# A decoder network on one NeuronCore: in the last attention layer, the next scores are issued ahead of the product of weights and values, in 11 of 16 steps

## The chip, the cores and the metric

The kernel runs on one core of one Trainium2 chip. The metric is the time of one execution on the device in microseconds, the median of several runs. The weights are loaded from HBM within the time.

## The reference, cut to what matters

The network has 256 tokens of 1024 channels and four mixers: a layer of two windowed attentions, one of forgetting attention, both with MLPs, an mLSTM, and last a sparse attention (NSA) with 16 heads of 64 in 4 groups. The change lies in the last one. With 256 tokens its selected and its windowed branch see all earlier keys, so each is causal attention with its own keys and values; the third branch attends to 15 compressed blocks. Their outputs are weighted by gates, added, multiplied by silu(z) and put through `w_out`:

```python
p_cmp = masked_softmax(jnp.einsum('bsghd,bcgd->bghsc', q, k_cmp) * scale, cmp_mask)
...
    p = masked_softmax(jnp.einsum('bqghd,bkgd->bghqk', qb, kb) * scale, mask)
    return jnp.einsum('bghqk,bkgd->bqghd', p.astype(vb.dtype), vb)
...
o = gate[..., 0:1] * heads(o_cmp) + gate[..., 1:2] * heads(o_sel) + gate[..., 2:3] * heads(o_win)
return (o.reshape(B, S, NSA_INNER) * jax.nn.silu(z)) @ w_out
```

All is float32. The kernel takes large products as three in rounded halves (high by high, high by low, low by high), and the attention's small products in float32.

## The kernel before, in words

The engines run programs of their own and meet at semaphores. Nothing reorders them: the order of the work is the order in which `pe`, `act`, `dve` and `pool` of the class `Nsa` are written.

The attention is cut into N = 16 steps. Step i holds the pair of heads j = i // 2 and the branch b = i % 2, with keys in two tiles of 128. One step passes through these stations:

- S, `score` (L2319, matmuls at L2328) on TensorE: the products of queries and keys, 4 instructions. Each contracts over 64 channels, so it takes half of the array's rows, and the two heads take one half each. The result goes to two PSUM banks, `SETS[i % 2]`, out of which the turned weights of step i - 2 must have been copied.
- `mask` (L2785, L2792) on VectorE: scale, causal mask and row maximum. It waits for the scores and keeps the masked scores in `nsa_sc`.
- `exp` (L2581, L2587) on ScalarE, with the row sum.
- `scale` (L2796, L2800 and L2806) on VectorE: by the sum's reciprocal and the gate.
- T, `turn` (L2333, L2337) on TensorE: six 128 x 128 transposes by a product with the identity, into the same banks.
- `keep` (L2590, L2595) on ScalarE: the copy of the turned weights into `nsa_pt`.
- V, `values` (L2341, L2352) on TensorE: weights times values, 4 instructions on all 128 rows and 64 columns each. In an odd step one more product follows, C (L2356): the compressed branch of the same heads, from `nsa_pc` and `nsa_vcmp`, over 64 rows. It closes the sum of the pair, and signals `summed`.
- `full` (L2825, L2830) on VectorE: the pair's y times silu(z), then `high` (L2601) on ScalarE and `low` (L2832, L2834) on VectorE, which split it for the output product.

In iteration k of the loop TensorE issues T(k), small products of the compressed branch where k % 4 is 3 or 1, half a chunk of projections or of the output product (`slot_half`, L2359, the matmuls of L189 to L191), V(k), and S(k + 2). V(k) and S(k + 2) both need `keep` of step k. S of steps 4, 8 and 12 also needs the turned queries of its group (`q_ready`): q is copied out behind slots 1, 5 and 9 (L2562), a DMA exchanges its halves (`nsa_qtwo`), VectorE multiplies and adds (L2731, L2738), and GpSimd multiplies the other part (L2513).

Beside this, ScalarE rounds the raw weight chunks to their high half (L155) and VectorE subtracts to get the low half (L159, L183); of four chunks GpSimd does the first half (L2505). In iteration k ScalarE does `exp(k + 1)` and then `keep(k)`, except in steps 6 and 10, where `keep` goes first. VectorE begins iteration k with `mask(k + 1)`; at even k from 2 on the gate product `full(k // 2 - 1)` follows, but `full(6)` stands at the end of iteration 13, and `low` behind it, ahead of `mask(15)`. After the loop TensorE finishes the output product, whose first matmul (L189) needs `low(6)`. In iteration 14 the output product waits for `full(6)` too.

Of the kernel before, what the change touches and what calls it, by code (L numbers as in the profile page):

```python
# [85 lines left out]
def build(nc, x, chunks, small_in, const_in, even_in, ml_in, nsa_in, fnorm_in, out):  # L86
# [100 lines left out]
    def product(pe, dst, a_hi, a_lo, b_hi, b_lo, start, stop):  # L187

        pe.matmul(dst, a_hi, b_hi, start=start, stop=False)  # L189
        pe.matmul(dst, a_hi, b_lo, start=False, stop=False)  # L190
        return pe.matmul(dst, a_lo, b_hi, start=False, stop=stop)  # L191

    def channel_tile(pe, slot, half, dst, h_hi, h_lo, ready=None):

        for k in range(KT):
            if ready is not None:
                pe.wait_ge(ready, k + 1)
            cols = slice(k * CW + half * P, k * CW + half * P + P)
            last = product(pe, dst, w_hi[slot][:, cols], w_lo[slot][:, cols],
                           h_hi[:, k, :], h_lo[:, k, :], k == 0, k == KT - 1)  # L200
        return last
# [26 lines left out]
    class Norm:  # L228
# [37 lines left out]
        def pe(self, pe):  # L266
            pe.wait_ge(self.diag_ready, TT)
            for k in range(KT):
                for t in range(TT):
                    at = (k % 2) * S + t * P  # L270
                    last = pe.matmul(bank[4 + k // 2][:, at:at + P], xres[:, t, k * P:(k + 1) * P],
                                     self.diag[:, t, :], start=True, stop=True)
                if k % 2 == 1:
                    last.then_inc(self.turned, 1)
# [1800 lines left out]
    class Nsa:  # L2075
# [354 lines left out]
        def pe(self, pe):  # L2430
            c0, inp = self.c0, self.inp
            first, rest = range(0, WIDE_KT), range(WIDE_KT, KT)
            pe.wait_ge(lo_ready, c0 + 1)
            pe.wait_ge(inp.lo_done.sem, inp.lo_done.at(WIDE_KT))
            for half in range(2):
                self.in_tile(pe, self.KC, half, bank[half][:, 0:S], first)
            inp.pe(pe, 1, self.before.added)
            pe.wait_ge(lo_ready, c0 + 2)
            for half in range(2):
                self.in_tile(pe, self.VC, half, bank[2 + half][:, 0:S], first)  # L2440
            pe.wait_ge(inp.lo_done.sem, inp.lo_done.at(KT))
            for half in range(2):
                last = self.in_tile(pe, self.KC, half, bank[half][:, 0:S], rest)
            last.then_inc(chunk_used, 1)
            pe.wait_ge(self.diag_ready.sem, self.diag_ready.at(TT))
            for t in range(TT):
                last = pe.matmul(bank[4][:, t * P:(t + 1) * P], ones, self.diag[:, t, :], start=True, stop=True)
            last.then_inc(self.rows_done.sem, 1)
            for half in range(2):
                last = self.in_tile(pe, self.VC, half, bank[2 + half][:, 0:S], rest)  # L2450
            last.then_inc(chunk_used, 1)
            pe.wait_ge(self.c_kept.sem, self.c_kept.at(1))
            self.in_whole(pe, self.KS, 0)
            pe.wait_ge(self.const_loaded.sem, self.const_loaded.at(16))
            self.gates(pe)
            self.in_whole(pe, self.KW, 1)
            pe.wait_ge(self.rows_kept.sem, self.rows_kept.at(1))
            pe.wait_ge(self.raw_kept.sem, self.raw_kept.at(1))
            self.in_whole(pe, self.Q[0], 0)
            pe.wait_ge(self.raw_kept.sem, self.raw_kept.at(2))  # L2460
            self.in_whole(pe, self.Z[0], 1)
            self.compress(pe, 0)
            self.compress(pe, 1)
            self.turn_gates(pe)
            self.values_half(pe, 0, 0)
            self.turn_hidden(pe, 0)
            self.values_half(pe, 0, 1)
            self.turn_hidden(pe, 1)
            pe.wait_ge(self.k_ready.sem, self.k_ready.at(2))
            pe.wait_ge(self.k_swapped.sem, self.k_swapped.at(4))  # L2470
            self.score(pe, 0)
            self.values_half(pe, 1, 0)
            self.compressed_keys(pe)
            self.compressed_values(pe)
            self.values_half(pe, 1, 1)
            pe.wait_ge(self.z_kept.sem, self.z_kept.at(1))
            self.score_compressed(pe, 0, 1)
            pe.wait_ge(self.cmp_kept.sem, self.cmp_kept.at(2))
            self.score(pe, 1)
            for k in range(self.N):  # L2480
                self.turn(pe, k)
                if k % 4 == 3 and k < 12:
                    self.score_compressed(pe, k // 4 + 1, 0)
                if k % 4 == 1:
                    self.turn_compressed(pe, k // 4)
                self.slot_half(pe, k)
                self.values(pe, k)
                if k + 2 < self.N:
                    self.score(pe, k + 2)
            for t in range(TT):  # L2490
                self.out_half(pe, 2, t).then_inc(self.t_done.sem, 1)
                if t == 1:
                    pe.wait_ge(lo_ready, self.o0 + 4)
                if t == 0:
                    self.out_half(pe, 3, t).then_inc(self.t_done.sem, 1)
            for i in range(2):
                self.out_quarter(pe, 3, i).then_inc(self.t_done.sem, 1)
# [1141 lines left out]
```

## Time and profile before

| | us |
|---|---|
| median of 3 runs | 932.59 |
| lowest and highest | 932.19, 932.75 |
| the profiled execution's own time | 932.07 |
| its span, first to last instruction | 930.2 |
| PE busy | 918.2 (99%) |
| DVE, ACT, POOL busy | 605.9, 561.9, 100.6 |
| first and last score matmul of this layer (L2328) | 810.3, 903.1 |
| PE's share of the chain that ended last | 89% |

PE is TensorE's matmuls, PEld its weight loads, DVE VectorE, ACT ScalarE, POOL GpSimd, SP the queue that issues most DMAs. The granted clock is 0.999 of full speed over the span. In a timeline a row gives the start, the time from the first start to the last recorded end, the engine, line, operation, tiles and shapes, how many instructions are merged, and in brackets how long the engine sat idle before and what it waited for. A float32 matmul stands as two records, one for each pass. "64*128" is an array use of 64 rows and 128 columns. The recorded ends of matmuls overlap the next starts, so distances are read from start to start.

### The profile page before, as it was taken

The numbers are of one execution on the slowest core, as the hardware profiler recorded it, in microseconds if no ns is written. First come the engines' busy times: TensorE is split into PE (matmuls) and PEld (weight loads), VectorE is DVE, ScalarE is ACT, GpSimd is POOL, SyncE is SP. The second block draws the span as 40 slices with busy tenths as digits, with TensorE's granted clock in tenths as the row PEclk, the third lists the DMA queues.
The fourth block names the chain that finished last, engine by engine and source line by source line (L and its number), as shares of the span: only waits on it lengthen the run. The fifth ranks groups of instructions, "written<-read, shape, count | busy, mean of one in ns | idle before, by whom it ended". The sixth has DMA issues, their size and how long they took to land.

```text
span 930.2 us, 15087 instructions
## 1 busy us (share of the span) xinstructions
PE 918.2 (99%) x6098; PEld 802.4 (86%) x6098; DVE 605.9 (65%) x1073; ACT 561.9 (60%) x927; POOL 100.6 (11%) x145
## 2 busy tenths in 40 slices
PE   9999999999999999999999999999999999999997
PEld 7876899998888877799998888999988889988876
DVE  6767676654456666666665454677479757777885
ACT  6687565553435787755555343656487547868873
POOL 0210000000000000000000016245003101311101
PEclk9999999999999999999999999999999999999999
DMA  9833565565554435236555565234333542731201
GB/s 362 322 139 125 181 213 194 182 213 194 181 184 173 149 128 181 69 142 228 197 182 212 195 221 184 95 130 140 138 139 106 227 172 99 266 118 53 99 24 46
DMA packets 23020, 153.57 MB, mean 165 GB/s; under 512 B 2632, under 2 KB 2888, under 8 KB 5544
## 3 DMA queue, kind: packets, MB, share of 16 engines
q1 hardware_dynamic: 22024, 149.17, 44.7%
q0 software_dynamic: 640, 3.15, 1.0%
q8 instruction: 48, 0.79, 0.3%
q10 hardware_dynamic: 288, 0.30, 0.1%
q14 instruction: 20, 0.16, 0.1%
HBM read 150.57 MB, written 1.05 MB: 163 GB/s over the span
## 4 chain that ended last, share of the span: by engine, by line
PE 89%; ACT 4%; DVE 4%; issue 1%; DMA 1%; SPq 0%; ACTq 0%; DVEq 0%
PE bank L189 26%; PE bank L191 25%; PE bank L190 25%; PE bank L931 1%; PE bank L2337 1%; PE bank L955 1%; PE bank L944 1%; PE bank L1610 1%; PE bank L2328 1%; PE bank L2352 1%; DVE w_hi_lo L159 1%; PE bank L761 1%; PE bank L1595 1%; ACT w_hi_lo L155 1%; DMA raw<-in_chunks 1%
## 5 line engine op out<-in xcount | busy, mean ns | idle before, releaser
L159 DVE TENSOR_TENSOR w_hi_lo<-raw,w_hi_lo 128x2048 fp32r<-128x2048 f32 x121 | 277.4, 2296 | 151.2 <-ACT w_hi_lo L155 151.1
L155 ACT ACTIVATE w_hi_lo<-raw 128x2048 fp32r<-128x2048 f32 x135 | 257.8, 1913 | 108.8 <-PE bank L191 107.4
L189 PE MATMUL bank<-h,w_hi_lo 128*128 128x256 f32 x960 | 270.0, 281 | 0.2 <-DVE ml_x L1872 0.2
L190 PE MATMUL bank<-h,w_hi_lo 128*128 128x256 f32 x960 | 266.2, 277 | 0.0
L191 PE MATMUL bank<-h,w_hi_lo 128*128 128x256 f32 x960 | 266.1, 277 | 0.0
L190 PEld LDWEIGHTS bank<-h,w_hi_lo 128*128 128x128 f32 x960 | 181.0, 188 | 0.4 <-issue 0.2
L189 PEld LDWEIGHTS bank<-h,w_hi_lo 128*128 128x128 f32 x960 | 180.4, 188 | 1.1 <-issue 0.7
L191 PEld LDWEIGHTS bank<-h,w_hi_lo 128*128 128x128 f32 x960 | 180.4, 188 | 0.0
L189 PE MATMUL bank<-w_hi_lo,mlp_u_hi 128*128 128x512 f32 x256 | 99.8, 390 | 0.0
L190 PE MATMUL bank<-w_hi_lo,mlp_u_hi 128*128 128x512 f32 x256 | 99.6, 389 | 0.0
L191 PE MATMUL bank<-w_hi_lo,mlp_u_lo 128*128 128x512 f32 x256 | 99.6, 389 | 0.0
L189 PE MATMUL bank<-w_hi_lo,h 128*128 128x512 f32 (+1 forms) x184 | 72.7, 395 | 0.3 <-DVE w_hi_lo L3354 0.3
L190 PE MATMUL bank<-w_hi_lo,h 128*128 128x512 f32 (+1 forms) x184 | 70.2, 381 | 0.0
L191 PE MATMUL bank<-w_hi_lo,h 128*128 128x512 f32 (+1 forms) x184 | 70.2, 381 | 0.0
L1214 ACT ACTIVATE mlp_work<-bank 128x256 f32<-128x256 f32 x64 | 21.1, 382 | 71.6 <-PE bank L191 71.6
L191 PEld LDWEIGHTS bank<-w_hi_lo,mlp_u_lo 128*128 128x128 f32 x256 | 48.1, 188 | 9.9
L189 PEld LDWEIGHTS bank<-w_hi_lo,mlp_u_hi 128*128 128x128 f32 x256 | 48.1, 188 | 9.9
L190 PEld LDWEIGHTS bank<-w_hi_lo,mlp_u_hi 128*128 128x128 f32 x256 | 48.1, 188 | 9.8
L769 ACT ACTIVATE h<-bank,small 128x256 fp32r<-128x256 f32 x48 | 18.8, 476 | 43.9 <-PE bank L761 43.9
L189 PEld LDWEIGHTS bank<-w_hi_lo,h 128*128 128x128 f32 x184 | 34.6, 188 | 10.5 <-issue 3.9
L191 PEld LDWEIGHTS bank<-w_hi_lo,h 128*128 128x128 f32 x184 | 34.6, 188 | 6.9
L190 PEld LDWEIGHTS bank<-w_hi_lo,h 128*128 128x128 f32 x184 | 34.7, 188 | 5.7
(397 smaller groups left out, 1434.2 us busy)
## 6 DMA issues: line engine op xcount, KB each, us to landing
raw<-in_chunks SPq DMA_DIRECT2D x136, 1024.0 KB, 4.9
even_bias<-in_even POOLq DMA_DIRECT2D x8, 384.0 KB, 3.4
xres<-in_x SPq DMA_DIRECT2D x2, 512.0 KB, 5.3
raw<-in_chunks SPq DMA_DIRECT2D x2, 512.0 KB, 6.4
ml_z<-in_ml SPq DMA_DIRECT2D x1, 896.0 KB, 5.8
nsa_qtwo<-nsa_qraw SPq DMA_DIRECT2D x8, 80.0 KB
small<-in_small SPq DMA_DIRECT2D x1, 559.5 KB, 11.9
final_gain<-in_fnorm SPq DMA_DIRECT2D x1, 512.0 KB, 3.6
```

Of the source, the lines that this page charges most:

```text
L155: act.activation(w_hi[slot][:, :], raw[slot][:, :], ACT.Copy).then_inc(hi_ready, 1)
L159: dve.tensor_tensor(w_lo[slot][:, :], raw[slot][:, :], w_hi[slot][:, :].bitcast(F32), ALU.subtract).then_inc(lo_ready, 1)
L189: pe.matmul(dst, a_hi, b_hi, start=start, stop=False)
L190: pe.matmul(dst, a_hi, b_lo, start=False, stop=False)
L191: return pe.matmul(dst, a_lo, b_hi, start=False, stop=stop)
L761: last = pe.transpose(self.spot(k)[:, t * P:(t + 1) * P], xres[:, t, k * P:(k + 1) * P], ident)
L769: act.activation(self.h[:, k, 0, :], self.spot(k), ACT.Copy, scale=self.gain[:, k:k + 1])\
L931: last = pe.matmul(bank[at_bank[e]][:, self.PS[t]:self.PS[t] + self.KEYS[t]], b["q"][half, t * P:(t + 1) * P], b["k"][half, 0:self.KEYS[t] ...
L944: last = pe.transpose(bank[self.banks_of[i % 2][e]][:, m * P:(m + 1) * P], self.sc[i % 2][:, e, at:at + P], ident)
L955: last = pe.matmul(dst[HALVES[e], kt * P:S], b["v"][e][kt], pt[:, e, kt * S:kt * S + S - kt * P], start=(kt == 0), stop=(kt == 1))
L1214: act.activation(self.z[n % 2][:, half * S:(half + 1) * S], self.up_bank(n, half)[:, 0:S], ACT.Copy).then_inc(self.z_ready.sem, 1)
L1595: last = pe.matmul(bank[5 + e][:, t * VW:(t + 1) * VW], self.X[:, j, t * P:(t + 1) * P], bdv[e][:, :], start=True, stop=True)
```

## The change

In iterations with k % 4 other than 2 and k + 2 < 16, S(k + 2) is issued ahead of V(k), behind a wait for the copy of step k. In iterations 2, 6 and 10, and in 14 and 15, the order stays. The other engines' programs are the same.

```diff
@@ -2484,9 +2484,14 @@
                 if k % 4 == 1:
                     self.turn_compressed(pe, k // 4)
                 self.slot_half(pe, k)
-                self.values(pe, k)
-                if k + 2 < self.N:
+                if k % 4 != 2 and k + 2 < self.N:
+                    pe.wait_ge(self.pt_ready.sem, self.pt_ready.at(k + 1))
                     self.score(pe, k + 2)
+                    self.values(pe, k)
+                else:
+                    self.values(pe, k)
+                    if k + 2 < self.N:
+                        self.score(pe, k + 2)
             for t in range(TT):
                 self.out_half(pe, 2, t).then_inc(self.t_done.sem, 1)
                 if t == 1:
```

TensorE at the end of iteration 1, from the end of slot 1 to the turn of step 2, before (each row an instruction, with the semaphores it waits for; `at_pt` is the copied weights, `ns_pc` the copied compressed weights, `at_scaled` the scaled ones):

```order
L191 MATMUL bank<-h,w_hi_lo 128x256
L2352 MATMUL bank<-nsa_pt,nsa_v 64x256 [waits at_pt]
L2352 MATMUL bank<-nsa_pt,nsa_v 64x256
L2352 MATMUL bank<-nsa_pt,nsa_v 64x128 x2
L2356 MATMUL bank<-nsa_pc,nsa_vcmp 128x256 [waits ns_pc]
L2328 MATMUL bank<-nsa_kd,nsa_qr 128x128 [waits at_pt]
L2328 MATMUL bank<-nsa_kd,nsa_qr 128x128
L2328 MATMUL bank<-nsa_kd,nsa_qr 128x256 x2
L2337 MATMUL bank<-small,nsa_sc 128x128 [waits at_scaled]
L2337 MATMUL bank<-small,nsa_sc 128x128 x5
```

The same place on TensorE now:

```order
L191 MATMUL bank<-h,w_hi_lo 128x256
L2328 MATMUL bank<-nsa_kd,nsa_qr 128x128 [waits at_pt]
L2328 MATMUL bank<-nsa_kd,nsa_qr 128x128
L2328 MATMUL bank<-nsa_kd,nsa_qr 128x256 x2
L2352 MATMUL bank<-nsa_pt,nsa_v 64x256 [waits at_pt]
L2352 MATMUL bank<-nsa_pt,nsa_v 64x256
L2352 MATMUL bank<-nsa_pt,nsa_v 64x128 x2
L2356 MATMUL bank<-nsa_pc,nsa_vcmp 128x256 [waits ns_pc]
L2337 MATMUL bank<-small,nsa_sc 128x128 [waits at_scaled]
L2337 MATMUL bank<-small,nsa_sc 128x128 x5
```

The scores moved past the values and past the compressed product, which now stands between the values and the turn; both still wait for the same copy, and the added wait gives no instruction of its own.

The second place is VectorE's program at the end of iteration 13 and the start of 14, which the change leaves as it is: the last scaling of step 14, half a chunk, the gate product `full(6)`, `low(5)`, and the mask of step 15 (`at_summed` is what V and C signal, `at_scores` what S signals):

```order
L2806 TENSOR_SCALAR nsa_sc<-nsa_sc,nsa_st,nsa_gate 128x256 x2
L183 TENSOR_TENSOR w_hi_lo<-raw,w_hi_lo 128x1024 [waits hi_ready]
L2830 TENSOR_TENSOR nsa_yf<-bank,nsa_sz 128x256 [waits at_ylo,ns_zready,at_summed]
L2834 TENSOR_TENSOR nsa_y_lo<-nsa_yf,nsa_y_hi 128x256 [waits at_yhi]
L2792 ISA nsa_sc,nsa_st<-bank,const 128x128 [waits at_turned,at_scores]
```

Nothing moved here, but on TensorE what `at_scores` stands for comes earlier and what `at_summed` stands for comes later.

## Rows read from the trace of the kernel before

**Rows 1.** The page, busy time, share of the span and instructions of TensorE

```profile
PE 918.2 (99%) x6098; PEld 802.4 (86%) x6098; DVE 605.9 (65%) x1073; ACT 561.9 (60%) x927; POOL 100.6 (11%) x145
```

**Rows 2.** Waits, 808 to 918 us: who waited for whom, us, times, longest

```profile
DVE nsa_sc L2792 <- PE bank L2328: 11.2, 11, 3.6
...
PE bank L2337 <- DVE nsa_sc L2806: 3.0, 3, 1.2
```

**Rows 3.** Timeline of TensorE, step 0: start us, us, engine line op

```profile
822.78 0.28 PE L190 MATMUL bank<-h,w_hi_lo 128*128 128x256 f32 x1
822.89 0.28 PE L191 MATMUL bank<-h,w_hi_lo 128*128 128x256 f32 x1
823.10 0.87 PE L2352 MATMUL bank<-nsa_pt,nsa_v 128*64 128x256 f32 x8
823.90 0.93 PE L2328 MATMUL bank<-nsa_kd,nsa_qr 64*128 64x128 f32 x8
824.76 0.87 PE L2337 MATMUL bank<-small,nsa_sc 128*128 128x128 f32 x6
```

**Rows 4.** Timeline of TensorE, steps 13 and 14

```profile
901.33 0.87 PE L2352 MATMUL bank<-nsa_pt,nsa_v 128*64 128x256 f32 x8
...
902.45 0.38 PE L2356 MATMUL bank<-nsa_pc,nsa_vcmp 64*128 64x256 f32 x1
...
906.96 0.87 PE L2352 MATMUL bank<-nsa_pt,nsa_v 128*64 128x256 f32 x8
907.76 0.88 PE L2337 MATMUL bank<-small,nsa_sc 128*128 128x128 f32 x6
```

**Rows 5.** Timeline of TensorE, step 1

```profile
829.63 0.48 PE L2356 MATMUL bank<-nsa_pc,nsa_vcmp 64*128 64x256 f32 x1
829.64 0.48 PE L2328 MATMUL bank<-nsa_kd,nsa_qr 64*128 64x128 f32 x2
...
830.91 0.87 PE L2337 MATMUL bank<-small,nsa_sc 128*128 128x128 f32 x6
```

**Rows 6.** Timeline of TensorE, step 15 and the output product behind it

```profile
912.24 0.70 PE L2356 MATMUL bank<-nsa_pc,nsa_vcmp 64*128 64x256 f32 x2
912.99 0.47 PE L189 MATMUL bank<-w_hi_lo,nsa_y_hi 128*128 128x512 f32 x1
```

**Rows 7.** Timelines of ScalarE, VectorE and TensorE ahead of steps 7 and 3

```profile
855.70 0.81 ACT L2595 ACTIVATE nsa_pt<-bank 128x768 f32<-128x768 f32 x1 [0.34 <-PE bank L2337]
856.53 1.28 ACT L2587 ACT_TABLE_LOAD   x1
...
861.24 0.87 PE L2337 MATMUL bank<-small,nsa_sc 128*128 128x128 f32 x6 [1.17 <-DVE nsa_sc L2806]
...
832.71 1.65 DVE L2731 TENSOR_TENSOR nsa_qtwo<-nsa_qtwo,nsa_csr 128x512 f32<-128x512 f32 x1 [0.48 <-DMA nsa_qtwo<-nsa_qraw]
...
836.91 0.88 PE L2337 MATMUL bank<-small,nsa_sc 128*128 128x128 f32 x6 [0.69 <-DVE nsa_sc L2806]
```

**Rows 8.** Timeline of VectorE, steps 13 to 15

```profile
903.10 0.42 DVE L2830 TENSOR_TENSOR nsa_yf<-bank,nsa_sz 128x256 f32<-128x256 f32 x1
...
903.76 0.29 DVE L2792 CUSTOM_DVE_ANT_0 nsa_sc<-bank,const 128x128 f32<-128x128 f32 x1
...
911.28 1.23 DVE L183 TENSOR_TENSOR w_hi_lo<-raw,w_hi_lo 128x1024 fp32r<-128x1024 f32 x1 [2.69 <-POOL w_hi_lo L2505]
912.42 0.42 DVE L2834 TENSOR_TENSOR nsa_y_lo<-nsa_yf,nsa_y_hi 128x256 fp32r<-128x256 f32 x1
```

**Rows 9.** Timelines of ScalarE and GpSimd, steps 14 and 15

```profile
905.87 0.79 ACT L2595 ACTIVATE nsa_pt<-bank 128x768 f32<-128x768 f32 x1
...
906.87 1.90 ACT L155 ACTIVATE w_hi_lo<-raw 128x2048 fp32r<-128x2048 f32 x1
...
908.84 2.40 POOL L2505 TENSOR_TENSOR w_hi_lo<-raw,w_hi_lo 128x1024 fp32r<-128x1024 f32 x1 [26.95 <-ACT w_hi_lo L155]
```

**Rows 10.** Timeline of TensorE's weight loads, the load of T in step 1

```profile
824.75 0.64 PEld L2337 LDWEIGHTS bank<-small,nsa_sc 128*128 128x128 f32 x6 [0.33 <-issue]
```

## The prediction

> **What bounds the kernel.** I read the page first: TensorE has a matmul in flight for 99% of the span [rows 1], and where it is busy throughout, only two things can change the time: the time of its own instructions, and the places where it waits. So the second view is the list of waits over the last stage. The change hopes for the first of its two rows: VectorE waited 11.2 us, in 11 places, for scores (L2328). But the row below it is the one that counts: TensorE itself waited for scaled weights (L2806) only 3 times, 3.0 us in all [rows 2]. VectorE's other waits are idle time of an engine with room to spare. The third view is TensorE's timeline at the block borders, because the edit alters only the order of three blocks: S (scores, L2328), V (weights times values, L2352, and in odd steps one product more, L2356, which I call C) and T (turning the next step's weights, L2337).
>
> **Even steps.** In step 0, V starts at 823.10, S at 823.90, T at 824.76 [rows 3]: from V's start to what follows it 0.80, from S's start to what follows it 0.86. These pitches include the change of block. If they belong to the block that goes before, as the same 0.80 from V straight to T in step 14 says (906.96 to 907.76, [rows 4]), S, V, T takes 0.86 + 0.80, what V, S, T took. Four of the 11 swapped steps are even (0, 4, 8, 12): price 0. If the pitch depended on the pair, the bounds would be the differences between these rows, 0.06 either way per step.
>
> **Odd steps.** Here C stood between V and S, and the records interleave: C starts at 829.63, S at 829.64, and T at 830.91 [rows 5]. C and S together take 1.28, S alone 0.86, so C costs 0.42 beside S. In the new order C stands between V and T. T uses all 128 rows of the array, C and each score 64. What C costs alone is seen in step 15, where nothing of S is left: it starts at 912.24 and the record of its two passes ends at 912.94 [rows 6]. T starts 0.07 before the recorded end of the 64-row block ahead of it (823.90 + 0.93 = 824.83 against 824.76, [rows 3]), so C alone takes 0.63: 0.21 more than beside S. The upper bound is the start of the next matmul, 912.99, hence 0.75 and 0.33 more, though that one also waits for VectorE (below). The lower bound is 0.42, no loss. I take 0.205, as the next matmul's own start is disturbed and the pass pair's end is not. The waits do not add to it: S now waits for the copied weights first (ScalarE, L2595) and V, which waited for the same copy, comes behind. A doubled wait on one semaphore is one wait, and no engine gets an instruction more.
>
> The Trainium skill, TensorEngine Tiling (Array Packing), section Key Properties, says that changing the tiling mode drains TensorE, and that different tiles may run in parallel. By it the odd steps have four mode changes between slot and T where they had three; at a price like the pitch from V to S less a normal one this would be about 0.1 per step, and the sum would be 0.5 us lower; that is an estimate. The trace says more than a drain: C alone against C beside S is 0.21 [rows 5, 6].
>
> **What the earlier scores buy.** S starts 0.80 sooner in even steps and 1.2 sooner in odd ones. This pays only where a T waits, in steps 3, 7 and 11. Take T(7): TensorE waited 1.17 for it and began at 861.24. Back from there: scaling, on the exponentials of step 7, behind a table load (856.53), behind ScalarE's copy of step 6's turned weights, from 855.70, which itself waited 0.34 for T(6) [rows 7]. The scores of step 7 are in none of these links. T(6) stands behind S and V in either order, so T(7) moves with T(6). T(11) repeats this. T(3), at 836.91, hangs on VectorE's product of 832.71 (L2731), which waited for the DMA that turns q [rows 7], and q is copied out behind slot 1, ahead of S and V. Gain: 0 in all three. It is also why the loss of step 1 costs nothing: T(3) starts at its time whatever happens in TensorE within its slack of 0.7. Should every score's lead reach T, the gain is bounded by 3.0 [rows 2].
>
> Steps 3, 5, 7, 9 and 11 keep their loss, as the waits behind them hang on T(6) and T(10), which are late too: 5 x 0.205 = 1.03 us.
>
> **The tail.** Here V's lateness meets an engine without slack. In step 13 VectorE multiplies y by the gate (L2830) at 903.10, just after the last product C of step 13 (V starts at 901.33; C's second pass ends at 902.45 + 0.38 = 902.83), and only behind it masks step 15's scores at 903.76 [rows 4, 8]. In the new order V starts at 901.33 + 0.86 = 902.19, C at 902.99, its second pass 0.32 later (912.94 - 0.38 - 912.24), at 903.31, with its end at 903.69. The gate product begins at about 903.73, 0.63 later, with the earlier scores of step 15 waiting behind it. All that follows is a chain: mask, exponentials, the copy of step 14 (905.87), rounding of the last weights (906.87), GpSimd's half of them (908.84 for 2.40), VectorE's other half (911.28), the low part of y (912.42), and TensorE's L189 at 912.99 [rows 6, 8, 9]. The output product of step 14 waits for the gate product too, and should just get it in time. On VectorE and GpSimd these stand back to back, so L189 moves from 912.99 to about 913.60, by 0.61. TensorE on its own would be later by 0.205 from step 13 and 0.2 from waiting for the copy of step 14 (906.96 + 0.205 against 907.36): 0.41 on 912.87, thus not the later of the two. From 912.99 on TensorE works through to the last blocks. Bounds: 0.2 (only C's loss) and 0.85 (the whole lead of S, 0.86).
>
> **Sum.** 1.03 + 0.61 = 1.64 us. On the profiled execution's 932.07 that is 933.7; its time is 0.52 below the median of 932.59, and on the median it is 934.2. A difference of 0.2% (1.87 us) is about what a measurement of this kernel tells from none; the forecast lies just inside, at 0.18%.
>
> **Rivals.** *C is dearer (0.12).* If C alone costs 0.75, each of the five steps loses 0.33 and the sum is 5 x 0.33 + 0.61 = 2.2 us: 934.8, slower by 0.24%. For it speaks the gap to 912.99, against it that VectorE's last row ends at 912.84, which leaves only its signal before 912.99. It decides from a price of 0.252 per step on: 5 x 0.252 + 0.61 = 1.87.
>
> *The tail is hidden (0.14).* ScalarE's chain before step 13 starts up to 0.8 earlier, and if some of that reached the mask of step 15, only 0.2 of the tail is left: 933.8; with no loss for C it is 932.8. Against it is the order of VectorE's rows: the mask stands behind the product that needs V.
>
> *The scores do pay (0.06).* If the waits of steps 3, 7 and 11 all vanish, -3.0 + 1.64 gives 931.2; without a loss for C, 930.2. Against it are the links of [rows 7].
>
> *Changes of block are free (0.04).* If TensorE loaded the next block's weights beside the running one, C alone would take two passes at the 0.11 pitch of the slot's matmuls of 256 columns (822.78 to 822.89, [rows 3]), 0.2 less than beside S, and every odd step would win 0.2: -1.0 + 0.4, 932.0. In the trace the weight load of T stands idle for 0.33 us before it starts behind S [rows 10]. The Trainium skill, TensorE: Matmul & The Clock Gate, section Step-by-step: what each phase is for, says that weight loads are pulled ahead of running matmuls when they go to the background buffer; that idle row says that here they are not.
>
> **How the numbers follow.** The forecast has 0.64, with a spread of its own of 933.7 to 934.7: a quarter of that, 0.17, is past 934.46 and counts as slower; with the first rival 0.29. Faster by over 0.2% (below 930.7) is only the last part of the third rival: 0.03. The rest, 0.68, is within 0.2%. The range reaches down to the second rival's end, 932.8, with 0.2 for the measurement, and up to the upper price with a longer tail, 5 x 0.33 + 0.85 = 2.5, 935.1.
>
> **What would show it.** Right: from slot to T about 2.5 us in odd steps (V, C and S took 2.08) with C alone between V and T, even steps unchanged at 1.66 to 1.67; waits before T(3) shorter by 0.2, before T(7) and T(11) as before; VectorE idle before L2830 in step 13, and about 0.6 us idle on TensorE or its weight load around steps 14, 15 and the L189 behind them; VectorE's waits for scores fewer. Wrong: T(7) or T(11) without a wait, C at 0.42 in its new place, or the mask of step 15 at its old distance from T(14).

## The result: 0.16% slower, and the profile after

| | before | after |
|---|---|---|
| median, us (22 runs each, same chip) | 932.45 | 933.90 |
| lowest and highest | 931.73, 932.90 | 933.45, 934.53 |
| ratio of the times, with its 95% interval | | 1.0016 [1.0010, 1.0022] |
| the profiled execution's own time | 932.07 | 933.72 |
| its span | 930.2 | 931.9 |

The difference of the medians is 1.45 us, that of the profiled executions 1.65; the forecast was 1.64, within 0.2%.

The page of the kernel after, busy time by engine [rows 1]; the granted clock is 0.998 over the span:

```profile
PE 919.8 (99%) x6098; PEld 801.9 (86%) x6098; DVE 605.9 (65%) x1073; ACT 561.6 (60%) x927; POOL 99.3 (11%) x145
```

The same instructions on every engine; TensorE's busy time is 1.6 longer, and the others' is the same within 1.3. Behind the edit all line numbers are 5 higher (VectorE's mask is L2797, its scaling L2811, the gate product L2835; ScalarE's copy L2600, its exponentials L2592). The waits of the kernel after, 808 to 920 us [rows 2]:

```profile
DVE nsa_sc L2797 <- PE bank L2328: 7.1, 8, 3.6
...
PE bank L2337 <- DVE nsa_sc L2811: 2.9, 3, 1.2
...
DVE nsa_yf L2835 <- PE bank L2356: 1.6, 2, 1.3
```

A row gives the total, how often, and the longest wait. The change does what it is for: VectorE waits for scores 7.1 us in place of 11.2. And it brings nothing: TensorE still waits 3 times for scaled weights, 2.9 in place of 3.0. A new wait has come, the gate product's for C, 1.3 at its longest.

TensorE of the kernel after, step 0, then step 1 [rows 3, 5]:

```profile
823.17 0.93 PE L2328 MATMUL bank<-nsa_kd,nsa_qr 64*128 64x128 f32 x8
824.03 0.87 PE L2352 MATMUL bank<-nsa_pt,nsa_v 128*64 128x256 f32 x8
824.83 0.87 PE L2337 MATMUL bank<-small,nsa_sc 128*128 128x128 f32 x6
...
828.90 0.93 PE L2328 MATMUL bank<-nsa_kd,nsa_qr 64*128 64x128 f32 x8
829.75 0.87 PE L2352 MATMUL bank<-nsa_pt,nsa_v 128*64 128x256 f32 x8
830.55 0.70 PE L2356 MATMUL bank<-nsa_pc,nsa_vcmp 64*128 64x256 f32 x2
831.18 0.87 PE L2337 MATMUL bank<-small,nsa_sc 128*128 128x128 f32 x6
```

The even step takes 1.66 from its first block to the turn, as before. The odd one takes 2.28 (before 2.08), and C by itself 0.63, to the hundredth what was read from step 15 [rows 6].

The turns that waited before, T(3), T(7) and T(11), in TensorE's timeline of the kernel after [rows 7]:

```profile
836.99 0.88 PE L2337 MATMUL bank<-small,nsa_sc 128*128 128x128 f32 x6 [0.54 <-DVE nsa_sc L2811]
...
861.72 0.87 PE L2337 MATMUL bank<-small,nsa_sc 128*128 128x128 f32 x6 [1.18 <-DVE nsa_sc L2811]
...
886.44 0.88 PE L2337 MATMUL bank<-small,nsa_sc 128*128 128x128 f32 x6 [1.18 <-DVE nsa_sc L2811]
```

T(3) waits less (0.54 in place of 0.69) and absorbs what step 1 lost. T(7) and T(11) wait as long as before.

The tail in TensorE's timeline of the kernel after [rows 4, 6]:

```profile
902.38 0.93 PE L2328 MATMUL bank<-nsa_kd,nsa_qr 64*128 64x128 f32 x8
903.23 0.87 PE L2352 MATMUL bank<-nsa_pt,nsa_v 128*64 128x256 f32 x8
904.03 0.70 PE L2356 MATMUL bank<-nsa_pc,nsa_vcmp 64*128 64x256 f32 x2
904.66 0.88 PE L2337 MATMUL bank<-small,nsa_sc 128*128 128x128 f32 x6
...
908.38 0.87 PE L2352 MATMUL bank<-nsa_pt,nsa_v 128*64 128x256 f32 x8
...
914.66 0.47 PE L189 MATMUL bank<-w_hi_lo,nsa_y_hi 128*128 128x512 f32 x1 [0.31 <-DVE nsa_y_lo L2839]
```

VectorE's and ScalarE's timelines there [rows 8, 9]:

```profile
904.77 0.42 DVE L2835 TENSOR_TENSOR nsa_yf<-bank,nsa_sz 128x256 f32<-128x256 f32 x1 [1.33 <-PE bank L2356]
...
905.44 0.28 DVE L2797 CUSTOM_DVE_ANT_0 nsa_sc<-bank,const 128x128 f32<-128x128 f32 x1
...
907.54 0.79 ACT L2600 ACTIVATE nsa_pt<-bank 128x768 f32<-128x768 f32 x1
...
912.96 1.22 DVE L183 TENSOR_TENSOR w_hi_lo<-raw,w_hi_lo 128x1024 fp32r<-128x1024 f32 x1 [2.69 <-POOL w_hi_lo L2510]
914.10 0.42 DVE L2839 TENSOR_TENSOR nsa_y_lo<-nsa_yf,nsa_y_hi 128x256 fp32r<-128x256 f32 x1
```

VectorE sits idle for 1.33 with the scores of step 15 in PSUM, because the gate product ahead of their mask waits for C. V(14) waits for the copy at 907.54, and L189 for the low part at 914.10.

**Where the 1.6 us came from.** T(k), S(k) and V(k) are the blocks of step k. A comparison of whole times mixes the change with what the rest of the program does in one execution; the part ahead of T(0), which no kernel here touches, comes out up to 1.0 us longer or 0.4 shorter from one profile to the next. So the table gives each block's start less its start in the kernel before, less the same difference of T(0); "L189" is the first output product behind step 15. Starts of before: T(0) 819.56, T(3) 836.91, T(7) 861.24, T(11) 885.57, T(12) 892.10, T(14) 903.41, T(15) 907.76, L189 912.99, end of the span 930.24. The runs of the next section stand in it too.

| kernel | T(0) starts | T(3) | T(7) | T(11) | T(12) | T(14) | T(15) | L189 | end |
|---|---|---|---|---|---|---|---|---|---|
| after | 819.63 | 0.00 | 0.40 | 0.80 | 1.00 | 1.18 | 1.36 | 1.60 | 1.60 |
| only even steps | 820.07 | 0.00 | 0.00 | 0.01 | 0.01 | 0.01 | 0.01 | -0.01 | -0.03 |
| only step 13 | 820.54 | 0.00 | -0.01 | -0.01 | -0.01 | 0.25 | 0.43 | 0.66 | 0.67 |
| all but step 13 | 819.12 | 0.00 | 0.40 | 0.80 | 1.00 | 0.97 | 0.97 | 0.85 | 0.86 |
| after, mask of 15 first | 819.83 | 0.00 | 0.39 | 0.79 | 0.99 | 1.17 | 1.21 | 1.09 | 1.11 |
| C, S, V in odd steps | 820.44 | -0.01 | -0.01 | -0.01 | -0.01 | -0.03 | 0.15 | 0.40 | 0.38 |
| V, S, C in odd steps | 820.02 | 0.01 | 0.01 | 0.00 | 0.00 | 0.00 | 0.18 | 0.42 | 0.40 |
| even: half S, V, half S | 819.67 | 0.21 | 0.41 | 0.61 | 0.60 | 0.79 | 0.79 | 0.67 | 0.68 |
| C, S, V, mask of 15 first | 819.55 | 0.00 | 0.00 | -0.01 | -0.02 | -0.02 | 0.37 | 0.24 | 0.25 |
| the same, exponentials first | 819.90 | -0.34 | -1.56 | -2.57 | -2.36 | -1.93 | -1.55 | -1.68 | -1.66 |
| before, exponentials first | 820.27 | -0.34 | -1.25 | -1.95 | -1.74 | -1.74 | -1.74 | -1.74 | -1.77 |
| the best combination | 819.70 | -0.33 | -1.53 | -2.53 | -2.32 | -2.32 | -2.32 | -2.40 | -2.44 |

For after: five steps of 0.20 make 1.00 up to T(12), and the tail adds 0.60.

### The profile page after: what moved, and what is told of

The parts are those of the page before. It is cut to its first block, busy times and chain, and to the rows that moved or that the text cites. A ratio compares the mean times of both kernels' runs of the same rounds, so it can differ in the third digit from the quotient of the medians.

```text
span 931.9 us, 15098 instructions
## 1 busy us (share of the span) xinstructions
PE 919.8 (99%) x6098; PEld 801.9 (86%) x6098; DVE 605.9 (65%) x1073; ACT 561.6 (60%) x927; POOL 99.3 (11%) x145
## 4 chain that ended last, share of the span: by engine, by line
PE 86%; issue 4%; ACT 4%; DVE 3%; DMA 1%; POOL 0%; POOLq 0%; SPq 0%; ACTq 0%; DVEq 0%
PE bank L189 25%; PE bank L191 24%; PE bank L190 24%; PE bank L931 1%; PE bank L955 1%; PE bank L944 1%; PE bank L1610 1%; DVE w_hi_lo L159 1%; PE bank L761 1%; PE bank L1595 1%; PE bank L2337 1%; ACT w_hi_lo L155 1%; DMA raw<-in_chunks 1%; PE bank L1587 1%; PE bank L2328 1%
## 5 line engine op out<-in xcount | busy, mean ns | idle before, releaser
L189 PE MATMUL bank<-h,w_hi_lo 128*128 128x256 f32 x960 | 270.0, 281 | 0.2 <-DVE ml_x L1872 0.2
L189 PEld LDWEIGHTS bank<-h,w_hi_lo 128*128 128x128 f32 x960 | 180.4, 188 | 1.1 <-issue 0.7
L189 PE MATMUL bank<-w_hi_lo,mlp_u_hi 128*128 128x512 f32 x256 | 99.8, 390 | 0.0
L189 PE MATMUL bank<-w_hi_lo,h 128*128 128x512 f32 (+1 forms) x184 | 72.7, 395 | 0.1
L189 PEld LDWEIGHTS bank<-w_hi_lo,mlp_u_hi 128*128 128x128 f32 x256 | 48.1, 188 | 9.9
L189 PEld LDWEIGHTS bank<-w_hi_lo,h 128*128 128x128 f32 x184 | 34.6, 188 | 10.4 <-issue 3.8
```

## The experiments

The theory: each odd step costs 0.2 because C is alone between V and T; the even steps cost nothing; step 13 costs 0.6 in all, through VectorE's order; and the early scores gain nothing because T(7) and T(11) hang on ScalarE's table load behind T(6) and T(10). The rivals: C's price comes from sharing lost with the scores or from a change of the array's use more; the tail is TensorE's own loss; the scores could pay if something else moved. All runs of the kernel before that are named here are from the same chip as the run they stand beside.

### Only the even steps

```diff
-                if k % 4 != 2 and k + 2 < self.N:
+                if k % 4 == 0 and k + 2 < self.N:
```

> Only the even steps 0, 4, 8 and 12 are swapped. Theory (C, the compressed product, costs 0.21 us more alone than beside the scores, plus a tail of 0.6 us behind step 13): no odd step is touched, so the time is that of the kernel before, within 0.2 us, and from the first scores to the turn behind them 1.66 us as before. Rival (each swap costs the same whatever stands around it, 1.5 us over 11 swaps): 4 x 0.14 = +0.5 us. Second rival (earlier scores pay a little everywhere and hide part of a larger loss): faster than before by 0.3 us or more.

Measured: 932.56 against 932.55, ratio 1.0001 [0.9992, 1.0010]. No block in the table moves by more than 0.01, and the end of the span by 0.03. The even steps cost nothing and gain nothing: S first takes 0.86 + 0.80, V first 0.80 + 0.86.

### Only step 13, and all but step 13

```diff
-                if k % 4 != 2 and k + 2 < self.N:
+                if k == 13:
```

> Only step 13 is swapped. Theory: +0.6 us, since the gate product of step 13 (VectorE, full(6)) waits for the later values, and the mask of step 15, the copy of step 14, the last rounding, GpSimd's and VectorE's halves and the low part of y follow back to back; VectorE idles about 1 us before full(6) and the first L189 behind step 15 starts 0.6 later against its turn of step 12. Rival (each swap costs the same, 0.14): +0.14 us. Second rival (the tail is as any odd step): +0.2 us.

```diff
-                if k % 4 != 2 and k + 2 < self.N:
+                if k % 4 != 2 and k < 13:
```

> All swaps but that of step 13. Theory: five odd steps (3, 5, 7, 9, 11) at 0.205 = +1.0 us, the swap of step 1 absorbed by the wait before the turn of step 3, and the tail as before. Rival (each swap costs the same): 10 x 0.14 = +1.4 us. Second rival (the whole loss sits in the tail): 0.

Measured: step 13 alone 933.07 against 932.55, ratio 1.0007 [0.9998, 1.0016], and 0.67 at the end of the span; all but step 13 933.21 against 932.55, ratio 1.0008 [1.0000, 1.0017], and 0.86. Single steps are below what the times can tell, and the blocks tell them apart. Together the two are 1.53, and the change has 1.60. The second loses 1.00 up to T(12) and ends at 0.86: ahead of L189 TensorE used to wait for VectorE a little, and of the 0.97 that it is late by itself 0.12 went into that.

### The change, with the mask of step 15 ahead of the gate product

VectorE takes the mask of step 15 at the end of iteration 13, ahead of `full(6)`, and no longer at the head of iteration 14:

```diff
-                if k + 1 < self.N:
+                if k + 1 < self.N and k != 14:
                     self.mask(dve, k + 1)
...
                 if k == 13:
+                    self.mask(dve, 15)
                     self.full(dve, 6)
```

> The changed kernel, with VectorE's mask of step 15 moved ahead of the gate product and the low part at the end of iteration 13. Theory: the wait for the later values holds nothing urgent any more, so of the tail's 0.6 only C's 0.2 is left, less the 0.1 that the first L189 waited for VectorE in the kernel before: +1.0 + 0.1 = +1.1 us against before, 0.4 to 0.5 faster than the changed kernel. Rival (the tail's loss is TensorE's own, or the chain over GpSimd does not set the end): no gain on the changed kernel, +1.5 us against before.

Measured: 933.44 against 932.55, ratio 1.0002 [0.9983, 1.0022], an interval that tells nothing alone (one of the 33 runs of the kernel before took 942.67 and widens it); in the profile 1.11 at the end in place of 1.60. VectorE's timeline:

```profile
903.53 0.29 DVE L2797 CUSTOM_DVE_ANT_0 nsa_sc<-bank,const 128x128 f32<-128x128 f32 x1
...
904.95 0.42 DVE L2835 TENSOR_TENSOR nsa_yf<-bank,nsa_sz 128x256 f32<-128x256 f32 x1 [0.22 <-PE bank L2356]
```

T(0) starts 0.20 later here than in after; with that taken off, the mask starts at 903.33 in place of 905.44, and 0.5 of the tail's 0.6 is gone. What is left at L189, 1.09, is TensorE's own 1.21 at T(15) less the 0.12 of slack ahead of L189 that the kernel without step 13 showed. Most of the tail's cost, 0.5 of 0.6, is the order of two operations on VectorE.

### C ahead of the scores: C, S, V in odd steps

C opens next to S as before, V comes last, its two key tiles in reverse so that the full-width one closes the sum:

```diff
+                    if k % 2 == 1:
+                        self.compressed_first(pe, k)
                     self.score(pe, k + 2)
-                    self.values(pe, k)
+                    self.values(pe, k, k % 2 == 1)
...
-            for kt in range(TT):
+            for kt in (range(TT)[::-1] if added else range(TT)):
```

> The changed kernel, with the compressed product C put first in the swapped odd steps: C, S, V, so that C stands beside the scores again and V closes the sum. Theory: the odd steps lose nothing, every turn up to step 12 stands where it stood before, and only the tail is left, since V ends 0.4 later than V and C did: +0.4 us against before, 1.1 faster than the changed kernel. Rival (S ahead of V costs its 0.2 in odd steps whatever C does): +1.4 us.

Measured: 933.02 against 932.01, ratio 1.0009 [1.0000, 1.0018]. The 1.0 of the odd steps is gone (T(12) at -0.01). 0.38 is left at the end: the gate product of step 13 now waits for V as the last one, starts 0.39 later, and the mask with it. The median shows 1.0 more where the blocks show 0.38, and 0.38 lies inside the interval (0 to 1.7 us). In this profile the part ahead of T(0) was 0.88 longer, which no edit here explains, so I go by the blocks.

The same with the mask of step 15 first:

> As the kernel with C, S, V, and the mask of step 15 ahead of the gate product as well. Theory: both losses are gone and the first L189 behind step 15 does not wait for VectorE: -0.1 us against before, same by any measure. Rival (something third in the swap costs time): +0.4 us or more, with the turns of steps 4 to 12 late.

Measured: 932.43 against 932.01, ratio 1.0005 [0.9996, 1.0013]; 0.25 at the end where a small gain was expected. A miss. VectorE's gate product and TensorE's blocks around it:

```profile
903.82 0.42 DVE L2842 TENSOR_TENSOR nsa_yf<-bank,nsa_sz 128x256 f32<-128x256 f32 x1
```

```profile
903.38 0.87 PE L2337 MATMUL bank<-small,nsa_sc 128*128 128x128 f32 x6
904.39 0.47 PE L189 MATMUL bank<-w_hi_lo,nsa_y_hi 128*128 128x512 f32 x1
```

The output product starts 1.01 behind T(14), where it took 0.63 before (903.41 to 904.04). Its bank is free only when the gate product has read it (it waits for the signal of `full(6)`), and that stands behind the mask now and ends at 904.24. The wait moved from the mask to the output product. In the change with the mask first it stood between, at 0.67. The two take VectorE 1.5 us together (902.70 to 904.24), and neither of the two orders tried serves an early S as well as a sum that closes late.

### What C's price is: one change of the array's use

A change of use is a border between two blocks whose rows print another shape: 64\*128 for S and C, 128\*64 for V, 128\*128 for the slot and T. The order V, C, S, T of an odd step has three such borders from the slot to T, the changed order S, V, C, T has four.

First V, S, C, T in odd steps: three borders as before, with C in front of T.

```diff
                 self.values(pe, k)
                 if k + 2 < self.N:
                     self.score(pe, k + 2)
+                    if k % 2 == 1:
+                        self.compressed_last(pe, k)
```

> The kernel before, with only C moved in the odd steps 1 to 13: V, S, C, T in place of V, C, S, T. TensorE changes its array use as often as before (slot to V, V to S, C to T), but C is in front of T and behind the scores. If C costs more because it brings one change of array use more (slot to S, S to V, V to C, C to T in the changed kernel), the distance from the start of V to T stays at the 2.08 of the kernel before, or within 0.05 of it, in every odd step. If C costs more because it has to stand next to a block that shares no rows, or because the last matmul ahead of T always costs its full time, the distance grows by about 0.2. The gate product of step 13 waits for C in either case and with it the mask of step 15: on the time from T(14) to the first L189 behind step 15 I expect 0.3 to 0.6 more, and 0.3 to 0.6 on the whole by the first reading, 1.3 to 1.6 by the second.

And the scores in two halves around V in the even steps 0, 4, 8 and 12: no C in them, and four borders in place of three. The odd steps are as before.

```diff
-                if k % 4 != 2 and k + 2 < self.N:
+                if k % 4 == 0 and k + 2 < self.N:
                     pe.wait_ge(self.pt_ready.sem, self.pt_ready.at(k + 1))
-                    self.score(pe, k + 2)
+                    self.score(pe, k + 2, range(1))
                     self.values(pe, k)
+                    self.score(pe, k + 2, range(1, TT))
```

> No C in it: only in the even steps 0, 4, 8 and 12, the scores of the first key tile stand ahead of V and those of the second behind it (S0, V, S1, T), all odd steps as before. That is one change of array use more per even step and the same matmuls. If a change costs about 0.2 by itself, the distance from the first of these blocks to T grows from 1.66 to about 1.86 in each of the four, steps 4, 8 and 12 keep it and the whole is 0.5 to 0.6 later; step 0's is lost in the wait ahead of T(3). If only C next to scores counts and changes are free, all distances and the time stay as before, within 0.05.

TensorE's timeline, step 1 of the kernel with V, S, C:

```profile
829.29 0.87 PE L2352 MATMUL bank<-nsa_pt,nsa_v 128*64 128x256 f32 x8
830.09 0.93 PE L2328 MATMUL bank<-nsa_kd,nsa_qr 64*128 64x128 f32 x8
830.85 0.59 PE L2364 MATMUL bank<-nsa_pc,nsa_vcmp 64*128 64x256 f32 x2
831.38 0.87 PE L2337 MATMUL bank<-small,nsa_sc 128*128 128x128 f32 x6
```

TensorE's timeline, step 0 of the kernel with the scores in two halves:

```profile
823.22 0.49 PE L2328 MATMUL bank<-nsa_kd,nsa_qr 64*128 64x128 f32 x4
823.64 0.87 PE L2353 MATMUL bank<-nsa_pt,nsa_v 128*64 128x256 f32 x8
824.44 0.70 PE L2328 MATMUL bank<-nsa_kd,nsa_qr 64*128 64x256 f32 x4
825.07 0.88 PE L2338 MATMUL bank<-small,nsa_sc 128*128 128x128 f32 x6
```

With V, S, C the distance is 2.09 (before 2.08), and no T up to T(14) moves by more than 0.01. With the halves the even step takes 1.85 (before 1.66), no matmul added. So C costs what it costs beside the scores wherever it touches them, in front of T too, and a border more costs 0.2 with no C in it.

Can it be sharing all the same, C on one half of the rows beside a score on the other? In the kernel before the two do run side by side (829.63 and 829.64, [rows 5]), and together they take 1.28. In V, S, C the rows of S and of C no longer interleave, and together they take 1.29 (830.09 to 831.38). Running side by side saves nothing here. What C loses alone stands at its two ends: S to V takes 0.85 in step 1 of the kernel after (828.90 to 829.75) where S to C took 0.76 (830.09 to 830.85), and C to T takes 0.63 (830.55 to 831.18) where it took 0.53 (830.85 to 831.38). That is 0.1 on the way out of the block ahead and 0.1 inside C, whose two passes stand at 0.70 in place of 0.59.

The weight loads are idle at these borders, but their idle time is no measure of the price. First step 1 of the kernel after, then step 0 of the kernel with halves, then T(15) of the kernel before, behind V(14):

```profile
829.75 0.63 PEld L2352 LDWEIGHTS bank<-nsa_pt,nsa_v 128*64 128x64 f32 x8 [0.33 <-issue]
830.55 0.29 PEld L2356 LDWEIGHTS bank<-nsa_pc,nsa_vcmp 64*128 64x128 f32 x2 [0.17 <-issue]
831.18 0.64 PEld L2337 LDWEIGHTS bank<-small,nsa_sc 128*128 128x128 f32 x6 [0.33 <-issue]
```

```profile
824.44 0.30 PEld L2328 LDWEIGHTS bank<-nsa_kd,nsa_qr 64*128 64x128 f32 x4 [0.17 <-issue]
825.07 0.64 PEld L2338 LDWEIGHTS bank<-small,nsa_sc 128*128 128x128 f32 x6 [0.33 <-issue]
```

```profile
907.76 0.64 PEld L2337 LDWEIGHTS bank<-small,nsa_sc 128*128 128x128 f32 x6 [0.17 <-issue]
```

At each change of use the weight load stands idle: 0.33 behind a block that ends in 256 columns (S, C, the second half of the scores), 0.17 behind V, which ends in 128 columns, whether C, scores or T follow, and 0.12 behind the first half of the scores, which ends in 128 too (823.64 less 823.22 and the 0.30 of its loads). It goes with the block that ends, and not with entering or leaving 64 rows.

The times, one run each: 932.91 and 932.85, beside 932.06 for the kernel before. One run doesn't tell such differences; the blocks give 0.40 (all of it the gate product of step 13, expected 0.3 to 0.6) and 0.68. The second was expected at 0.5 to 0.6, since step 0's loss should have vanished in T(3)'s wait. It didn't: T(3) is 0.21 late. q is copied out behind slot 1, and a loss ahead of slot 1 delays q too: VectorE's product with the turned q starts 13.38 behind T(0) in place of 13.15. A loss in step 1, behind that slot, is absorbed.

### The exponentials ahead of the table load

If the early scores gain nothing because exp(7) and exp(11) stand behind ScalarE's copy of step 6 or 10, which waits for T(6) or T(10), and a table load behind it, moving them ahead of silu and its tables should free T(7) and T(11). Two engines change: ScalarE does the exponentials and the copy ahead of silu, and VectorE scales ahead of the gate product, where `k % 4 == 2`:

```diff
-                if k in self.KEEP_FIRST:
-                    self.keep(act, k)
-                if k + 1 < self.N:
-                    self.exp(act, k + 1)
                 if k not in self.KEEP_FIRST:
+                    self.exp(act, k + 1) if k + 1 < self.N else None
                     self.keep(act, k)
...
                     if 5 <= k < 12:
+                        self.exp(act, k + 2)
+                        self.keep(act, k + 1)
                         self.silu_z(act, k // 4)
...
                 if k % 4 == 2 and k < 12:
                     self.mul_q(dve, k // 4 + 1)
                     self.add_q(dve, k // 4 + 1)
+                if k % 4 == 2 and k < 12 and k not in ():
+                    self.scale(dve, k + 1)
...
-                if 1 <= k and k + 1 < self.N:
+                if 1 <= k and k + 1 < self.N and not (k % 4 == 2 and k < 12):
                     self.scale(dve, k + 1)
```

On top of C, S, V and the mask first:

> As the kernel before it, and now the three waits ahead of the turns of steps 3, 7 and 11 are attacked where they hang: ScalarE does the exponentials of steps 7 and 11 and the copy of steps 6 and 10 ahead of silu(z) and its table load, and VectorE scales steps 3, 7 and 11 ahead of the gate product. Theory (the waits hang on ScalarE's tables and VectorE's order, not on the scores): the wait of step 3 falls by 0.3, those of steps 7 and 11 from 1.2 to about 0.3 each: -2.2 us against before. Rival (the later silu or GpSimd's use of the port VectorE shares gives it back): 0 to -0.5 us.

And on the kernel before, with its order V, C, S:

> The same orders on ScalarE and VectorE, but TensorE in the order of the kernel before (V, C, S) and the mask of step 15 at its old place. Theory: the scores of step 7, 1.2 us later than in the kernel beside it, delay the exponentials and the copy of step 6 by about 0.8, which still ends 0.4 before V(6) needs it, and the scaling of step 7 is held by q's sum all the same: -2.1 us, as good as with early scores within 0.3 us. Rival (only with early scores can the exponentials go first): less than half of the gain, with waits ahead of V(6) and V(10).

Measured: 930.38 against 932.01, ratio 0.9982 [0.9973, 0.9991]; and 930.67 against 932.01, ratio 0.9986 [0.9977, 0.9994]. ScalarE's timeline of the first:

```profile
854.44 0.40 ACT L2599 ACTIVATE nsa_sc<-nsa_sc,nsa_st 128x128 f32<-128x128 f32 x1 [1.03 <-DVE nsa_st L2803]
...
856.22 0.79 ACT L2607 ACTIVATE nsa_pt<-bank 128x768 f32<-128x768 f32 x1
857.02 1.28 ACT L2591 ACT_TABLE_LOAD   x1
```

TensorE at T(7), of the second:

```profile
860.71 0.88 PE L2337 MATMUL bank<-small,nsa_sc 128*128 128x128 f32 x6 [0.25 <-DVE nsa_sc L2805]
```

In the first, T(7) follows S without a wait. Both kernels beat the one before (by 1.6 and 1.3 us in the medians), and both fall short of what was expected (2.2 and 2.1), by the blocks (1.66 and 1.77) by 0.5 and 0.3. Three things follow.

- Most of the 3.0 us of waits [rows 2] was the order on ScalarE and VectorE, and comes back without early scores. The two engines were moved together, so how much belongs to which was not tested, but for T(3), where only VectorE's order differs: 0.34.
- Once the exponentials are out of the table's shadow, early scores do pay: T(7) gains 1.56 against 1.25, T(12) 2.36 against 1.74.
- With the early scores the first one loses 0.8 of that again, between T(12) and T(15), in step 13. Its rows say where:

```profile
899.76 0.45 PE L2344 MATMUL bank<-nsa_pc,nsa_vcmp 64*128 64x256 f32 x1 [0.39 <-ACT nsa_pc L2586]
```

C stands first in step 13, and TensorE waits 0.39 there for the copy of the compressed weights; T(14) has lost 0.43. The other 0.4 is lost up to T(15), where the output product waits behind the gate product as it did in the kernel with C, S, V and the mask first (1.00 behind T(14) here, 1.01 there).

### The best combination

So: the exponentials first, C, S, V in odd steps up to 11, and step 13 and VectorE's iteration 13 as in the kernel before (`k % 4 != 2 and k < 13`, no mask moved), which takes away both waits of step 13.

> The orders of the run with the exponentials moved ahead (ScalarE: exponentials of steps 7 and 11 and the copies of steps 6 and 10 ahead of silu; VectorE: scaling of steps 3, 7 and 11 ahead of the gate product), with C, S, V in odd steps up to 11, but step 13 in the order of the kernel before (V, C, S) and VectorE's end of iteration 13 as before too. That run had gained 2.36 at T(12) and only 1.66 at the end; if the 0.7 was lost because step 13's new order holds up the gate product or what stands behind it, this kernel keeps 2.3 to 2.4 to the end: 0.9975 of the kernel before. If the 0.7 was lost to something that was hidden at first (a DMA, GpSimd's half chunk), it ends at 1.7 again, 0.9982.

Measured: 929.67 against 932.06, ratio 0.9973 [0.9963, 0.9983]: the fastest of all. TensorE's waits for scaled weights, 808 to 918 us, and VectorE's step 13:

```profile
PE bank L2337 <- DVE nsa_sc L2817: 0.4, 1, 0.4
```

```profile
900.85 0.42 DVE L2841 TENSOR_TENSOR nsa_yf<-bank,nsa_sz 128x256 f32<-128x256 f32 x1
...
901.52 0.28 DVE L2803 CUSTOM_DVE_ANT_0 nsa_sc<-bank,const 128x128 f32<-128x128 f32 x1
```

Of three waits one is left, of 0.4, at T(3), where q's DMA bounds it. The gate product and the mask follow the work ahead of them with no idle time. T(12)'s 2.32 is kept, and the end has 2.44.

## Why the prediction was right

- **Even steps, price 0**: right, 1.66 before and after, and 0.01 when they change alone.
- **Odd steps, 0.205 each**: right in size, 0.20 at T(2), T(4), T(6), T(8), T(10) and T(12), step 1's absorbed at T(3). Right for a reason that the prediction put second. It read the price as sharing lost with S and set it above what a change of use by itself would give. V, S, C and the halved scores speak for the change of use: 0.00 where C moved and the count did not, 0.20 where the count grew and no C moved, and side by side with S or behind it C costs the same. So the size, read from step 15, was well founded, and the cause named for it was not. The Trainium skill, TensorEngine Tiling (Array Packing), section Key Properties, says that switching the mode requires a drain; the runs agree in that each further switch costs, 0.20, and do not show what it consists of. The estimate of 0.1 that the prediction hung on that page was half of the price, since it took only the way out of a block and left out the 0.1 inside the block that follows. The sign "from slot to T about 2.5 us" was a slip: the prediction's own terms give 0.86 + 0.80 + 0.63 = 2.29, and 2.28 was measured.
- **The gain, 0**: right. T(7) and T(11) waited 1.18 each (before 1.17 at T(7)), and moving the exponentials and the scaling took their wait away with early scores, and all but 0.25 of T(7)'s without.
- **The tail, 0.61**: 0.60. The gate product was forecast 0.63 later; it came 0.60 later (904.77 less 903.10, less the 1.00 of the steps ahead and the 0.07 of T(0)). The two paths are as told: V(14) waits for the copy of 907.54, TensorE's T(15) is 1.36 late, and L189, held by VectorE, 1.60. Taking the mask ahead of the gate product removed 0.5 of it.
- **The rivals.** *C is dearer*: no, 0.63 alone. *The tail is hidden*: no, VectorE idled 1.33 with the scores of step 15 already there. *Changes of block are free*: no, by the halved scores. Its price for C was also too low: the 0.11 is the pitch of the slot's rounded operands, and C, in float32, takes two records of about 0.21 each even without a border in front of it (0.76 + 0.53 = 1.29 less 0.86). *The scores pay*: not here, though 0.6 of them (2.32 less 1.74 at T(12)) pays when the order on ScalarE and VectorE and C's place change with them; the prediction did not see that this rival lacked only a neighbour's order.
- **The sum** of 1.64 stands against 1.60 in the profile and 1.45 in the medians, whose interval reaches from 0.9 to 2.1.

## What to carry to other kernels

An engine that waits often for something is no reason to bring that thing earlier; follow the wait that the busiest engine has back through every link, and move what stands in one of them. When a block is moved, count the changes of array use before and after, and ask for each operation behind it in the queues whether it now waits for the block that became the last. An edit that brings nothing alone can pay beside another: the early scores did when the table load was out of their way, C stayed beside S and the one step without slack was left as it was.

## What the runs showed of the hardware

- One more border between blocks of another array use costs about 0.20 us for float32 matmuls, measured on two different blocks (2.28 against 2.08 with C, 1.85 against 1.66 with the halved scores). In both cases the added border sets one more 64-row block between blocks of 128 rows; other additions were not measured. About half is lost on the way out of the block ahead and half inside the 64-row block. The weight load is idle for 0.12 to 0.33 at such a border, according to the block that ends.
- C, two passes of 256 columns, costs 0.42 wherever it touches a block of the same use (1.28 and 1.29 with S, on either side of it), and 0.63 between two others. Running on one half of the rows while a score runs on the other saves nothing against running behind it.
- The stretch ahead of T(0), the same in all kernels here, varied by 1.4 us between profiles (819.12 to 820.54), as much as the whole effect. Start times taken from a block ahead of the change agree to 0.03 wherever two kernels do the same, and tell what medians of 11 runs can't.
